# Hybrid decoder block: the state-space scan with channels on the partitions, and its norm applied after the output product

## The chip, the cores and the metric

One NeuronCore of a Trainium2 chip runs the whole program. Its engines are TensorE (PE in the rows), VectorE (DVE), ScalarE (ACT), GpSimd (POOL) and SyncE (SP, which issues most DMAs). The metric is the time on the device in microseconds (us) for one execution, the median of several runs.

## The reference

One decoder layer over 512 positions with a width of 1024: a norm, one projection `w_in` to the columns of three mixers (a convolution, a sparse attention, a state-space scan), their outputs side by side through `w_out`, a residual add, a second norm and a feed-forward part. Only the scan is touched. Its reference, cut to what matters:

```python
CHUNK = 128   # 4 chunks; 8 heads of 64 channels; 2 groups of B and C; state 128
xd  = xh * dt[..., None]
cs  = cumsum(dt * a) within the chunk
scores = (C[l] . B[s]) * exp(cs[l] - cs[s])          # l >= s, per head
y_diag = einsum("bclsh,bcshp->bclhp", scores, xd)
y_off  = einsum("bclhn,bchpn,bclh->bclhp", C, state_before_chunk, exp(cs))
y = y_diag + y_off + d_skip[:, None] * xh
y = rms_norm(y.reshape(S, 512) * silu(z), ssm_norm_g)   # mean over the 512 channels
x = x + concat([conv, att, y], -1) @ w_out
```

## The kernel before, in words

Everything is float32. The large products are done in three passes of a rounded part (`_hi`) and its rest (`_lo`): weight high by input high, weight high by input low, weight low by input high (`product`, L1767). A weight of 128 by 2048 numbers is a "chunk"; ScalarE makes `w_hi` of it (L934) and VectorE `w_lo` (L640), in two slots that alternate.

The order of work is one list, `PLAN`, made by `make_plan`. It has four "slots" for each of the 23 chunks before the feed-forward part. A slot begins with TensorE's 12 matmuls of a quarter of a chunk (`mg`), and the plan puts small steps at fixed slots. Every engine walks the same list and does its part of each step, so that its instructions stay in that order; semaphores join the engines. In a slot, the steps of `front` stand first, then those of `put`, then those of `fill`.

The scan takes one chunk of 128 positions (t = 0 to 3) each four slots, from n = 68, 72, 76 and 80 (`SSD_SLOTS`). The steps of one chunk are:
- `csr` (n): TensorE spreads the running sum `cs` over the partitions, four heads in a bank (bfloat16, L2000 and L2005).
- `seg` (n+1): ScalarE takes `dec` = exp of it, eight instructions of 128x128 (L1099). GpSimd makes `xd`, `xskip` (the D skip term) and `xdd` (L887 to L892).
- `ssd` (n+1): TensorE makes the product of B and C (`gt2`, L2014) and turns B round (`bt`, L1773).
- `sct` (n+2): VectorE makes the scores, `gt2` by `dec` (L1463).
- `yd` (n+2): TensorE multiplies scores and `xd` (L2031): for each head the 128x128 scores are the stationary operand and 64 columns of `xd` move, so that positions come out on the partitions. From t = 1 on it multiplies C and `state` (`yo`, L2039), and up to t = 2 it makes the next state (`st`, L2047).
- `ssdout` (n+3): VectorE scales `yo` by exp(cs), adds `yd` and `xskip`, multiplies by silu(z) (L1490) into `yb`, and updates `state`.
- `ysq`, `yms` (n+3, n+4), `yn`: ScalarE sums the squares along each row with an accumulator (L1114), VectorE and GpSimd make the inverse root, and VectorE scales `yb` by it and by the norm's gain `gssm` (L1512).
- `yT`, `ssdT` (n+5, n+6): TensorE turns `yb` so that channels are on the partitions (L1773), ScalarE takes `ssm_hi` (L922) and VectorE `ssm_lo` (L1519).

From slot 68 to 91 the large products are those with `w_out`: att in two halves, conv in two halves, ssm in two halves, four `mg` each. VectorE adds each to the residual `x2` (step `wo`, L1575), and the second norm follows. `z`, the gate of the scan, is projected in slots 60 to 67 with `h` stationary, two chunks of four k tiles each, positions on the partitions.

Results pass through eight PSUM banks. Four (`acc`) serve the large products, three (`aux`) the small steps in rotation, one (`out`) `pv` and `yd`. A step claims its bank, and waits until the group that had it before has been drained:

```python
        def claim(eng, *key):
            if RING[key][3]:
                eng.wait_ge(drained[RING[key][2]], RING[key][3])
```

## Time and profile before

| | us |
|---|---|
| median of 3 runs | 717.45 (717.26 to 717.74) |
| the profiled execution | 717.7 |
| its span in the profile | 716.0 |
| TensorE busy | 697.0 (97%) |
| VectorE busy | 545.4 (76%) |
| ScalarE busy | 380.6 (53%) |
| GpSimd busy | 141.8 (20%) |

The span is the time from the first to the last instruction of the profile; 1.7 us of the execution lie around it. The granted TensorE clock is full in all 40 slices of the page. The scan lies between about 275 and 352 us of the span, the feed-forward part begins at about 371 us.

A matmul of float32 operands stands in the trace as two records, so that eight of them are "x16". Matmuls are pipelined: the duration of one is longer than the distance to the next, and what a group of them takes is read from one start to the next.

### The profile page before, as it was taken

The page shows a single profiled execution, that of the slowest core. Times are in us where ns is not written, and L with a number is a line of the kernel's source. Part 1 is how long each engine was busy: PE and PEld are TensorE (multiplying, and loading weights), DVE is VectorE, ACT ScalarE, POOL GpSimd, SP SyncE. Part 2 cuts the span into 40 slices and gives each one's busy share as a digit, 9 for nine tenths or more (in the row PEclk, how much of TensorE's full clock was granted, in tenths as well). Part 3 has the DMA queues.
Part 4 walks back from the last instruction along what each step waited for, and adds up shares of the span by engine and source line. Part 5 has one row for each costly group of instructions (what it writes and reads, how often), then busy time and mean ns, then how long its engine had stood idle before and what let it go on. Part 6 is the DMA issues. An engine that isn't in the chain of part 4 may idle for free.

```text
span 716.0 us, 9787 instructions
## 1 busy us (share of the span) xinstructions
PE 697.0 (97%) x3402; PEld 560.4 (78%) x3402; DVE 545.4 (76%) x852; ACT 380.6 (53%) x570; POOL 141.8 (20%) x114
## 2 busy tenths in 40 slices
PE   4999999999999999999999999999999999999998
PEld 4776888667666788788888888888888888888886
DVE  4368989988898947667667777876766866997895
ACT  6254655988878765633464343343343343654660
POOL 2000477944564402233410000000000000000000
PEclk9999999999999999999999999999999999999999
DMA  8731314211111141312234588656687547864552
GB/s 245 235 127 60 118 59 117 62 60 59 59 60 60 59 177 61 135 70 60 59 118 140 173 246 249 190 170 200 186 249 237 179 160 298 297 221 140 169 162 88
DMA packets 87554, 104.09 MB, mean 145 GB/s; under 512 B 6871, under 2 KB 65591, under 8 KB 87519
## 3 DMA queue, kind: packets, MB, share of 16 engines
q1 hardware_dynamic: 87375, 103.12, 45.9%
q10 hardware_dynamic: 144, 0.52, 0.2%
q8 instruction: 20, 0.33, 0.2%
q14 instruction: 15, 0.12, 0.1%
HBM read 87.10 MB, written 16.54 MB: 145 GB/s over the span
## 4 chain that ended last, share of the span: by engine, by line
PE 87%; ACT 7%; DVE 4%; issue 2%; DMA 1%; POOL 0%; DVEq 0%; ACTq 0%
PE bank L1767 75%; PE bank L1773 4%; PE bank L1787 2%; ACT tapped L1129 1%; ACT w_hi L934 1%; PE bank L1975 1%; DVE u_acc L622 1%; PE bank L2031 1%; PE bank L1951 1%; DVE xbcT L1427 1%; PE bank L1926 1%; DMA x_in<-in_x 1%; ACT prob L1052 1%; ACT dec L1099 0%; DVE prob L1406 0%
## 5 line engine op out<-in xcount | busy, mean ns | idle before, releaser
L1767 PE MATMUL bank<-h_hi,w_hi 128*128 128x512 f32 (+1 forms) x496 | 192.9, 389 | 0.0
L1767 PE MATMUL bank<-h_lo,w_hi 128*128 128x512 f32 (+1 forms) x496 | 189.9, 383 | 0.0
L1767 PE MATMUL bank<-h_hi,w_lo 128*128 128x512 f32 (+1 forms) x496 | 189.8, 383 | 0.0
L1767 PEld LDWEIGHTS bank<-h_hi,w_hi 128*128 128x128 f32 x496 | 93.2, 188 | 25.7 <-issue 7.8
L1621 DVE SCALAR_TENSOR_TENSOR f<-bank,prm,f 128x511 f32<-128x511 f32 x88 | 65.8, 748 | 60.7 <-ACT f L1182 55.2
L1767 PEld LDWEIGHTS bank<-h_hi,w_lo 128*128 128x128 f32 x496 | 93.2, 188 | 18.4
L1767 PEld LDWEIGHTS bank<-h_lo,w_hi 128*128 128x128 f32 x496 | 93.3, 188 | 17.3
L860 POOL TENSOR_TENSOR u_acc<-tapped,u_acc 128x511 f32<-128x511 f32 (+29 forms) x60 | 90.1, 1502 | 46.1 <-ACT tapped L1129 43.0
L1182 ACT ACTIVATE f<-bank,prm 128x512 f32<-128x512 f32 x44 | 34.2, 777 | 70.4 <-PE bank L1767 70.2
L640 DVE TENSOR_TENSOR w_lo<-w_raw,w_hi 128x2048 fp32r<-128x2048 f32 x24 | 55.6, 2316 | 8.9 <-ACT w_hi L934 8.7
L1767 PE MATMUL bank<-w_hi,g_parts 128*128 128x512 f32 x168 | 53.8, 389 | 0.0
L1596 DVE TENSOR_TENSOR w_lo<-w_raw,w_hi 128x2048 fp32r<-128x2048 f32 x22 | 50.3, 2287 | 3.4 <-ACT w_hi L1171 3.4
L622 DVE SCALAR_TENSOR_TENSOR u_acc<-u_in,prm,u_acc 128x511 f32<-128x511 f32 (+29 forms) x60 | 51.9, 877 | 0.8
L1189 ACT ACTIVATE sg<-f 128x512 f32<-128x512 f32 x22 | 13.9, 632 | 72.4 <-DVE f L1621 72.4
L1129 ACT ACTIVATE tapped<-u_in,prm 128x511 f32<-128x511 f32 (+29 forms) x60 | 40.2, 704 | 21.4 <-POOL u_acc L860 15.5
L1767 PE MATMUL bank<-w_hi,h_hi 128*128 128x512 f32 x128 | 51.2, 400 | 0.0
L1767 PE MATMUL bank<-w_hi,h_lo 128*128 128x512 f32 x128 | 50.0, 390 | 0.0
L1767 PE MATMUL bank<-w_lo,h_hi 128*128 128x512 f32 x128 | 49.9, 390 | 0.0
L934 ACT ACTIVATE w_hi<-w_raw 128x2048 fp32r<-128x2048 f32 x24 | 45.8, 1910 | 3.5 <-DMA w_raw<-in_w_in 2.2
L840 POOL TENSOR_TENSOR stats<-stats 128x1 f32<-128x1 f32 (+1 forms) x24 | 23.1, 966 | 103.4 <-DVE stats L1507 35.1
L1171 ACT ACTIVATE w_hi<-w_raw 128x2048 fp32r<-128x2048 f32 x22 | 41.9, 1906 | 0.0
L1767 PEld LDWEIGHTS bank<-w_hi,g_parts 128*128 128x128 f32 x168 | 31.5, 188 | 6.6
(279 smaller groups left out, 1228.2 us busy)
## 6 DMA issues: line engine op xcount, KB each, us to landing
w_raw<-in_w_up SPq DMA_DIRECT2D x44, 512.0 KB, 6.1
w_raw<-in_w_in SPq DMA_DIRECT2D x34, 512.0 KB, 4.6
down_raw<-in_w_down SPq DMA_DIRECT2D x22, 512.0 KB, 5.4
weight_sums<-down_raw SPq DMA_DIRECT2D x11, 768.0 KB, 5.3
w_raw<-in_w_out SPq DMA_DIRECT2D x12, 512.0 KB, 4.5
weight_sums<-w_sum SPq DMA_DIRECT2D x11, 512.0 KB, 2.7
w_raw<-weight_sums SPq DMA_DIRECT2D x6, 768.0 KB, 6.0
down_raw<-weight_sums SPq DMA_DIRECT2D x5, 768.0 KB, 4.4
```

Of the source, the lines that this page charges most:

```text
L622: eng.scalar_tensor_tensor(out=u_acc[:, j, i:], in0=u_in[:, j, 0:SEQ - i], scalar=w, in1=u_acc[:, j, i:], op0=ALU.mult, op1=ALU.add).then_ ...
L640: eng.tensor_tensor(wlo[:, slot, cols], wraw[:, slot, cols], whi[:, slot, cols].bitcast(F32), ALU.subtract).then_inc(ready, 1)
L840: pool.tensor_tensor(out_, in_, half_neg[:, 0:n], ALU.pow).then_inc(ready, 1)
L860: pool.tensor_tensor(u_acc[:, j, i:], tapped[j][:, i % 4, 0:SEQ - i], u_acc[:, j, i:], ALU.add).then_inc(dw_taps[j], 1)
L934: act.activation(whi[:, c % NSLOT, :], wraw[:, c % NSLOT, :], ACT.Copy)\
L1129: act.activation(tapped[j][:, i % 4, 0:SEQ - i], u_in[:, j, 0:SEQ - i], ACT.Copy, scale=prm[:, c:c + 1]).then_inc(dwp_ready, 1)
L1171: act.activation(whi[:, c % NSLOT, :], wraw[:, c % NSLOT, :], ACT.Copy)\
L1182: act.activation(fbuf[:, 2 * s + v, :], bank[FFN_BANK[2 * s + v]][:, :], ACT.Identity, bias=prm[:, bass.ds(tile + R_FB, 1)], scale=prm[:, ...
L1596: dve.tensor_tensor(wlo[:, c % NSLOT, :], wraw[:, c % NSLOT, :], whi[:, c % NSLOT, :].bitcast(F32), ALU.subtract)\
L1621: ins = dve.scalar_tensor_tensor(out=fbuf[:, 2 * s + v, i:], in0=bank[FFN_BANK[2 * s + v]][:, 0:SEQ - i], scalar=prm[:, bass.ds(tile + (R_ ...
L1767: ins = pe.matmul(o, a, b, start=first and i == 0 and q == 0, stop=last and i == n - 1 and q == 2)
L1773: return pe.transpose(o, in_, ident[0:n, 0:n])
```

## The change

The scan is computed with channels on the partitions throughout, and the norm's factor, which belongs to a position, is applied later, where positions are on the partitions again.
- `yd`: `xd` of one head (128x64) is stationary and the scores (128x128) move. The two heads of a pair write the two halves of the bank's partitions. `yo`: `state` is stationary and C moves, four matmuls of 128 columns.
- `eb`, new from t = 1 on: TensorE spreads cs over the partitions of the channels (eight bfloat16 matmuls, 64 partitions by 128 columns), ScalarE takes exp of it into `ecs_rows`. This takes the place of the scaling by a column of `ecs`. Its bank is in the rotation of three.
- `xskip` is made by four GpSimd instructions of 128x128 from `xbcT`, no longer by one of 128x512; `dcol` (two small copies on VectorE) holds the factors.
- `z` is projected as two chunks of all eight k tiles, with `w` stationary, channels on the partitions. Its loads have rows of 256 numbers, not 512.
- `ysq`: ScalarE squares `yb` without an accumulator and takes `ssm_hi` = `yb` by the gain, from SBUF, four instructions (the gain is one number for each partition). `yred` (VectorE) sums the squares of the four channel tiles, `yq` (TensorE, 32 columns) sums over the partitions, `yms` (VectorE, GpSimd) makes the inverse root, one slot later than before. `ssm_lo` takes four instructions from SBUF.
- `yT`, `yn` and the turning are gone. The inverse root scales the ssm product at the residual add (`wo`, ssm), eight instructions.
- The gain arrives as four rows of `prm` instead of a row spread over all partitions.

The core of the diff:

```diff
-        put(n + 4, ("yms", t))
-        front[n + 5].append(("yn", t))
-        put(n + 5, ("yT", t))
-        front[n + 6].append(("ssdT", t))
+        front[n + 4] += [("yred", t), ("ssdT", t)]
+        put(n + 5, ("yq", t))
+        front[n + 6].append(("yms", t))
...
+            if s[1]:
+                aux.append(("eb", s[1]))
...
-            if what in ("iq", "xbc", "conv"):
+            if what in ("iq", "xbc", "z", "conv"):
...
-                    pool.tensor_tensor(sk3, v3, per_head(hbc[:, 2, :]), ALU.mult)\
-                        .then_inc(xd_ready, 1)
-                    pool.wait_ge(xd_ready, 3 * t + 1)
+                    for j in range(4):
+                        pool.tensor_scalar(xskip[:, P * j:P * j + P], xbcT[:, j, P * t:P * t + P],
+                                           dcol[:, j:j + 1], None, ALU.mult).then_inc(xd_ready, 1)
+                    pool.wait_ge(xd_ready, 6 * t + 1)
...
+                    if t:
+
+                        if t > 1:
+                            evacuated(act, "yo", t - 1)
+                        finished(act, "eb", t)
+                        drain(act.activation(ebc[:, :], ps("eb", t)[:, :], ACT.Exp), "eb", t)
...
-                    act.activation(dump[:, :], yb[:, :], ACT.Square,
-                                   accum_out=yss[:, t:t + 1]).then_inc(yss_ready, 1)
-                elif k == "ssdT":
-                    t = s[1]
-                    finished(act, "yT", t)
-                    high(ssm_hi[:, :, P * t:P * t + P],
-                         ps("yT", t)[:, :].rearrange("p (j q) -> p j q", j=4))
+                    act.activation(dump[:, :], yb[:, :], ACT.Square).then_inc(ysq_ready, 1)
+                    for j in range(4):
+                        act.activation(ssm_hi[:, j, P * t:P * t + P], yb[:, P * j:P * j + P], ACT.Copy,
+                                       scale=prm[:, R_SG + j:R_SG + j + 1]).then_inc(shi_ready, 1)
...
-                    dve.wait_ge(yss_ready, t + 1)
-                    dve.tensor_scalar(yss[:, t:t + 1], yss[:, t:t + 1], 1.0 / 512, EPS, ALU.mult,
-                                      ALU.add).then_inc(yms_ready, 1)
-                elif k == "yn":
-                    t = s[1]
-                    dve.wait_ge(yrs_ready, t + 1)
-                    dve.scalar_tensor_tensor(out=yb[:, :], in0=yb[:, :], scalar=yrs[:, t:t + 1],
-                                             in1=gssm[:, :], op0=ALU.mult, op1=ALU.mult)\
-                        .then_inc(yn_ready, 1)
+                    finished(dve, "yq", t)
+                    drain(dve.tensor_scalar(yss[:, t:t + 1], ps("yq", t)[:, 0:1], 1.0 / 512, EPS,
+                                            ALU.mult, ALU.add), "yq", t)
+                    evacuated(dve, "yq", t)
+                    dve.sem_inc(yms_ready, 1)
                 elif k == "ssdT":
                     t = s[1]
-                    wait_high(s)
+                    dve.wait_ge(shi_ready, 4 * t + 4)
                     q = slice(P * t, P * t + P)
-                    drain(dve.tensor_tensor(ssm_lo[:, :, q],
-                                            ps("yT", t)[:, :].rearrange("p (j q) -> p j q", j=4),
-                                            ssm_hi[:, :, q].bitcast(F32), ALU.subtract), "yT", t)
+                    for j in range(4):
+                        dve.scalar_tensor_tensor(
+                            out=ssm_lo[:, j, q], in0=yb[:, P * j:P * j + P],
+                            scalar=prm[:, R_SG + j:R_SG + j + 1], in1=ssm_hi[:, j, q].bitcast(F32),
+                            op0=ALU.mult, op1=ALU.subtract).then_inc(slo_ready, 1)
+                elif k == "yred":
+                    t = s[1]
+                    dve.wait_ge(ysq_ready, t + 1)
+                    dve.tensor_reduce(ysq_sum, dump[:, :].rearrange("p (j q) -> p q j", j=4),
+                                      AX_X, ALU.add).then_inc(yred_ready, 1)
...
-                    drain(dve.tensor_tensor(xx, ps(*s)[:, :], xx, ALU.add), *s)
+                    if g == "ssm":
+
+                        dve.wait_ge(yrs_ready, t + 1)
+                        drain(dve.scalar_tensor_tensor(out=xx, in0=ps(*s)[:, :],
+                                                       scalar=yrs[:, t:t + 1], in1=xx,
+                                                       op0=ALU.mult, op1=ALU.add), *s)
...
+                    if t:
+                        claim(pe, "eb", t)
+                        for j in range(4):
+                            for n in range(2):
+                                c = SH * t + 2 * j + n
+                                ins = pe.matmul(
+                                    ps("eb", t)[SP_ * n:SP_ * n + SP_, P * j:P * j + P],
+                                    sel3[:, c:c + 1].to_broadcast([96, SP_]), cs_rows[:, :],
+                                    start=True, stop=True)
+                        ins.then_inc(aux_done, 1)
...
-                        c = slice(SP_ * h, SP_ * h + SP_)
-                        ins = pe.matmul(ps("yd", t)[:, c], sct[:, h, :], xd[:, c], start=True,
+                        j, n = divmod(h, 2)
+                        ins = pe.matmul(ps("yd", t)[SP_ * n:SP_ * n + SP_, P * j:P * j + P],
+                                        xd[:, SP_ * h:SP_ * h + SP_], sct[:, h, :], start=True,
                                         stop=True)
...
+                elif k == "yq":
+                    t = s[1]
+                    pe.wait_ge(yred_ready, t + 1)
+                    claim(pe, "yq", t)
+                    pe.matmul(ps("yq", t)[:, 0:32], ysq_sum, ones[:, 0:32], start=True, stop=True)\
+                        .then_inc(aux_done, 1)
```

TensorE from `yd` of t = 1 to `yd` of t = 2, in the order before (the 24 matmuls of two slots, `csr`, and 12 and 12 more stand where rows are left out):

```order
L2031 MATMUL bank<-xd,sct 128x64 x8
L2039 MATMUL bank<-state,xbcT 128x256 x2
L2047 MATMUL bank<-xdd,b_tok 128x256 x2
...
L1773 MATMUL bank<-ident,yb 128x128 x4
L2014 MATMUL bank<-xbcT 128x128 x2
L1773 MATMUL bank<-ident,xbcT 128x128 x2
...
L2031 MATMUL bank<-xd,sct 128x64 x8
```

And in the order of the change (`cs_rows,sel_55` after `bt` is `eb`, `ones,stats` is `yq`):

```order
L2069 MATMUL bank<-sct,xd 64x128 x8
L2078 MATMUL bank<-xbcT,state 128x128 x4
L2086 MATMUL bank<-xdd,b_tok 128x256 x2
...
L2093 MATMUL bank<-ones,stats 128x32
L2042 MATMUL bank<-xbcT 128x128 x2
L1799 MATMUL bank<-ident,xbcT 128x128 x2
L2055 MATMUL bank<-cs_rows,sel_55 64x128 x8
...
L2069 MATMUL bank<-sct,xd 64x128 x8
```

The turning of `yb` gives way to one matmul, and the eight of `eb` are put in between `bt` and the next `mg`.

VectorE from the gate of t = 1 to the scores of t = 2, before (`x_115` is `x2`):

```order
L1490 TENSOR_TENSOR yb<-yb,z_tok 128x512
L1496 TENSOR_TENSOR state<-state,stats 128x512
L1500 TENSOR_TENSOR state<-bank,state 128x512
L1575 TENSOR_TENSOR x_115<-bank,x_115 128x512
L1507 TENSOR_SCALAR stats<-stats 128x1
L1575 TENSOR_TENSOR x_115<-bank,x_115 128x512
L1512 SCALAR_TENSOR_TENSOR yb<-yb,stats,gssm 128x512
L1575 TENSOR_TENSOR x_115<-bank,x_115 128x512
L640 TENSOR_TENSOR w_lo<-w_raw,w_hi 128x2048
L1519 TENSOR_TENSOR ssm_lo<-bank,ssm_hi 128x4x128
L1463 TENSOR_TENSOR sct<-bank,dec 128x512 x2
```

And in the change:

```order
L1506 TENSOR_TENSOR yb<-yb,z_tok 128x512
L1512 TENSOR_TENSOR state<-state,stats 128x512
L1516 TENSOR_TENSOR state<-bank,state 128x512
L1601 TENSOR_TENSOR x_115<-bank,x_115 128x512
L1539 TENSOR_REDUCE stats<-square_dump 128x128
L1532 SCALAR_TENSOR_TENSOR ssm_lo<-yb,prm,ssm_hi 128x128 x4
L1601 TENSOR_TENSOR x_115<-bank,x_115 128x512 x2
L645 TENSOR_TENSOR w_lo<-w_raw,w_hi 128x2048
L1523 TENSOR_SCALAR stats<-bank 128x1
L1480 TENSOR_TENSOR sct<-bank,dec 128x512 x2
```

`ssm_lo` has moved from between `w_lo` and `sct` to ahead of `w_lo`; `yms` (the TENSOR_SCALAR that reads a bank) stands behind `w_lo` and drains the bank of `yq`.

ScalarE from the square of t = 0 to `dec` of t = 1, before:

```order
L1114 ACTIVATE square_dump,stats<-yb 128x512
L1150 ACTIVATE u_tok<-bank,prm 128x4x128
L1155 ACTIVATE conv_hi<-u_tok 128x512
L1150 ACTIVATE u_tok<-bank,prm 128x4x128
L1155 ACTIVATE conv_hi<-u_tok 128x512
L934 ACTIVATE w_hi<-w_raw 128x2048
L1099 ACT_TABLE_LOAD
L1099 ACTIVATE dec<-bank,stats 128x128 x8
```

And in the change:

```order
L1129 ACTIVATE square_dump<-yb 128x512
L1131 ACTIVATE ssm_hi<-yb,prm 128x128 x4
L1164 ACTIVATE u_tok<-bank,prm 128x4x128
L1169 ACTIVATE conv_hi<-u_tok 128x512
L1164 ACTIVATE u_tok<-bank,prm 128x4x128
L1169 ACTIVATE conv_hi<-u_tok 128x512
L941 ACTIVATE w_hi<-w_raw 128x2048
L1106 ACT_TABLE_LOAD
L1106 ACTIVATE dec<-bank,stats 128x128 x8
```

The four instructions of `ssm_hi` are new in this stretch; they came after `dec`, as one, before.

## Rows read from the trace of the kernel before

**Rows 1.** The page: span; busy time and share of the engines.

```profile
span 716.0 us, 9787 instructions
PE 697.0 (97%) x3402; PEld 560.4 (78%) x3402; DVE 545.4 (76%) x852; ACT 380.6 (53%) x570; POOL 141.8 (20%) x114
```

**Rows 2.** Windows: stretch, then busy us of each engine, clock, DMA share, GB/s.

```profile
262.00:371.00 109.00, 107.15 (x596) 89.68 (x595) 76.02 (x117) 56.78 (x106) 31.68 (x28) 1.00 0.26 83
371.00:716.00 345.00, 341.76 (x1542) 284.09 (x1540) 260.68 (x324) 148.28 (x162) 0.00 (x0) 1.00 0.62 195
```

**Rows 3.** Timeline of TensorE, t = 0 and 1: start, us, what, [idle before].

```profile
283.56 0.39 PE L1767 MATMUL bank<-w_hi,att_lo 128*128 128x512 f32 x1
283.79 1.89 PE L2031 MATMUL bank<-xd,sct 128*128 128x64 f32 x16
285.52 1.08 PE L2047 MATMUL bank<-xdd,b_tok 128*128 128x256 f32 x4
...
298.83 0.44 PE L1773 MATMUL bank<-ident,xbcT 128*128 128x128 f32 x2 [0.32 <-ACT dec L1099]
...
301.63 0.39 PE L1767 MATMUL bank<-w_hi,att_lo 128*128 128x512 f32 x1
302.15 2.00 PE L2031 MATMUL bank<-xd,sct 128*128 128x64 f32 x16
303.98 1.08 PE L2039 MATMUL bank<-state,xbcT 128*128 128x256 f32 x4
304.90 1.03 PE L2047 MATMUL bank<-xdd,b_tok 128*128 128x256 f32 x4
...
316.00 0.48 PE L1767 MATMUL bank<-w_hi,conv_hi 128*128 128x512 f32 x1
```

**Rows 4.** Chain that ended last: start, us from this to the next, what.

```profile
249.19 1.02 PE bank L1975 x16
...
261.41 0.22 PE bank L1993 x2
...
311.64 0.23 PE bank L2005 x4
...
335.76 1.73 PE bank L2031 x16
...
346.63 0.44 PE bank L1773 x4
```

**Rows 5.** Timeline of ScalarE, from the first turned conv tile to `dec` of t = 1.

```profile
287.08 0.78 ACT L1150 ACTIVATE u_tok<-bank,prm 128x512 f32<-128x512 f32 x1 [2.23 <-PE bank L1773]
...
289.76 0.61 ACT L1114 ACTIVATE square_dump<-yb 128x512 f32<-128x512 f32 x1
...
290.71 0.78 ACT L1150 ACTIVATE u_tok<-bank,prm 128x512 f32<-128x512 f32 x1 [0.24 <-PE bank L1773]
...
295.31 1.28 ACT L1099 ACT_TABLE_LOAD   x1
296.60 2.17 ACT L1099 ACTIVATE dec<-bank,stats 128x128 f32<-128x128 f32 x8
```

**Rows 6.** Timeline of VectorE, t = 1 to 2.

```profile
305.17 0.69 DVE L1476 TENSOR_TENSOR yb<-bank,stats 128x512 f32<-128x512 f32 x1 [2.48 <-PE bank L2039]
...
312.74 2.53 DVE L640 TENSOR_TENSOR w_lo<-w_raw,w_hi 128x2048 fp32r<-128x2048 f32 x1
...
317.79 1.28 DVE L1463 TENSOR_TENSOR sct<-bank,dec 128x512 f32<-128x512 f32 x2
```

**Rows 7.** Groups of VectorE by shape: count, busy us, mean ns, idle before.

```profile
L1374 DVE TENSOR_REDUCE stats<-sq 128x8 f32<-128x512 f32 x8 | 5.4, 678 | 3.4 <-ACT sq L1021 3.4
L1512 DVE SCALAR_TENSOR_TENSOR yb<-yb,stats,gssm 128x512 f32<-128x512 f32 x4 | 5.3, 1332 | 0.2
L1547 DVE SCALAR_TENSOR_TENSOR x2n<-x,stats,gf_row 128x512 f32<-128x512 f32 x4 | 3.0, 749 | 0.8 <-POOL stats L840 0.7
```

**Rows 8.** Timelines of GpSimd (t = 1), VectorE and TensorE (the end of the stage).

```profile
293.74 1.49 POOL L892 TENSOR_TENSOR xdd<-xd,stats 128x512 f32<-128x512 f32 x1
...
356.85 0.68 DVE L1575 TENSOR_TENSOR x<-bank,x 128x512 f32<-128x512 f32 x1
...
362.34 1.09 PE L1773 MATMUL bank<-ident,x2n 128*128 128x128 f32 x8 [0.77 <-ACT x2n L1141]
```

More of the change, by code:

```diff
@@ L38 @@
 R_QG, R_KG = 96, 97
-N_ROW0 = 98
+R_SG = 98
+N_ROW0 = 102
 R_CW = N_ROW0
@@ L466, in build @@
                   2: at("tapped2", [P, 4, 512], F32, r1)}
-        gssm = at("gssm", [P, 512], F32)
+        ebc = at("ecs_rows", [P, 512], F32)
         dec = at("dec", [P, SH, P], F32, rs)
@@ L654, in load @@
                 done = w_landed[c % NSLOT]
-                if what in ("iq", "xbc"):
-                    c0 = C_IQ if what == "iq" else C_XBC + 256 * i
+                if what in ("iq", "xbc", "z"):
+                    c0 = {"iq": C_IQ, "xbc": C_XBC, "z": C_Z}[what] + 256 * i
                     src = w_in[:, c0:c0 + 256].rearrange("(k p) n -> p k n", p=P)
@@ L880, in _ @@
                     v3 = xs_tok[:, t, :].rearrange("p (h c) -> p h c", h=SH)
-                    x3, xx3, sk3 = (b_.rearrange("p (h c) -> p h c", h=SH)
-                                    for b_ in (xd[:, :], xdd[:, :], xskip))
+                    x3, xx3 = (b_.rearrange("p (h c) -> p h c", h=SH)
+                               for b_ in (xd[:, :], xdd[:, :]))
                     def per_head(ap):
@@ L1883, in _ @@
                             pe.wait_ge(pool_lo_ready, POOL_LO.index(c) + 1)
-                    if what in ("iq", "xbc", "conv"):
+                    if what in ("iq", "xbc", "z", "conv"):
                         key = ("cg" if q < 2 else "ca", i) if what == "conv" else \
@@ L1900, in _ @@
                         key, k0 = ("wo", g, half, q), 0
-                        if half == 0 and g != "conv":
-                            evacuated(pe, "pv" if g == "att" else "yT", q)
+                        if half == 0 and g == "att":
+                            evacuated(pe, "pv", q)
+                        elif half == 0 and g == "ssm":
+                            pe.wait_ge(slo_ready, 4 * q + 4)
                         elif (half, q) == (0, 0):
```

66 lines of the change are left out of this document (36 added, 30 removed).

## The prediction

> **What bounds the kernel now.** I read the page first: TensorE is busy for 697.0 of 716.0 us [rows 1], so time is won or lost where TensorE's instructions become fewer or shorter, or where it waits. Next the windows: the feed-forward part from 371 us on has 341.8 busy us in 345 and no step of the change; the stretch 262 to 371, where the scan lies, has 107.15 in 109 [rows 2]. So in this stage too TensorE is the engine that the others follow, and its waits make up under 2 us. Then the timelines of this stage, which show where these waits are. At t = 0 `yd` starts 0.23 us after the last large matmul, which is the usual distance. At t = 1 it starts 0.52 us after it, 0.29 late, and the group then takes 1.83 us to the start of `yo`, not 1.73: a wait costs 0.40 in all [rows 3]. What it waits for is `sct`; at t = 2 that ends at about 319.07, when TensorE starts `yd` at once [rows 6], so the wait is there twice (t = 1 and 2). A third is at 298.83, 0.32 us for `dec` of t = 1 [rows 3]. `dec` is late because ScalarE has worked almost without a break since 287.08: four conv tiles, a square, a `w_hi`, a table load, eight exps [rows 5].
>
> **The change on TensorE, start to start.**
> - `yd`: before, 16 records take 1.73 us [rows 4], 0.108 each although only 64 columns move. After, 64 columns are stationary, 128 move, and the heads alternate between the two halves of the output partitions. This form is in the trace: `pv` of the last block has 64 columns of `v_tok` stationary, 128 moving and alternating halves, and 16 records take 1.02 us [rows 4]. I take 1.02: minus 0.71 each. The bound from above is 1.73 (nothing gained).
> - `yo`: 4 records of 256 columns in 0.92 us (303.98 to 304.90, [rows 3]) become 8 of 128 at 0.11, the price of a turned tile (0.44 for four [rows 4]): 0.88. Minus 0.04.
> - `yT` 0.44 goes, `yq` comes: one matmul of 32 columns on 128 stationary ones, as L1993, 0.22 [rows 4]. Minus 0.22 each.
> - `eb`: eight bfloat16 matmuls of 128 columns, three times. Four of `csr` take 0.23 [rows 4], so at most 0.46; if the halves overlap as in `pv`, 0.27. I take 0.30.
> - `z`: 96 matmuls of 512 columns before and after, and the same bytes; `xbc` is projected in the new form already. Nothing, and its banks are claimed later than before. The load of `gssm` that goes is small and early. Nothing.
>
> **What it does to the waits.** `ssm_lo` no longer stands between `w_lo` and `sct`. Before, `w_lo` of t = 2 ends at 315.27 but `sct` starts only at 317.79 [rows 6], as `ssm_hi`, made from the turned tile, has to come first. After, `sct` needs `gt2` (at about 316) and ends near 317.3, a good microsecond before `yd`. So the 0.40 goes at t = 1 and 2.
>
> The wait for `dec` of t = 1 stays, and here the first chunk's gain is lost. ScalarE starts its stretch when TensorE has turned the first conv tiles (287.08, after `yd` of t = 0), now 0.71 earlier. It waits 0.24 at 290.71 [rows 5], which leaves; the accumulator's read (0.19) goes; four `ssm_hi` come, at the price of `dec`, 2.17 / 8 = 0.27 each [rows 5], 1.09. Sum: -0.71 - 0.24 - 0.19 + 1.09 = -0.05. So `dec` ends 0.05 earlier and TensorE goes on 0.05 earlier, whatever it had gained by `yd` and `yT` of t = 0.
>
> Step by step, TensorE against before:
> - start of `yd`(1): -0.05 + 0.30 (`eb`) - 0.29 (wait) = -0.04
> - to the end of `yo`(1): -0.10 (restart) - 0.71 - 0.04, hence -0.89
> - start of `yd`(2): -0.22 + 0.30 - 0.29, hence -1.10; end of `yo`(2): -1.95
> - t = 3, without a wait: -0.22 + 0.30 - 0.71 - 0.04, hence -2.62; `yq`(3) -0.22: -2.84
>
> **The new wait.** `eb`(t) gets the bank of `yq`(t-1), which is free only when VectorE has done `yms`, and that stands behind `w_lo` in its queue. Behind `eb` on TensorE stand the next 12 large matmuls, so each microsecond of lateness is a microsecond of the kernel. Before, from the start of `yb` (305.17) to the end of `w_lo` (315.27) are 10.1 us [rows 6]. Out go the scaling L1512 with its wait and the small operation, 1.65; in come `yred` (0.60 start to start, 0.68 busy as L1374 [rows 7]) and four `ssm_lo`. A quarter of a clean 512 wide instruction (0.75 [rows 7]) is 0.19, the whole is 0.75; near the lower end, as ScalarE's narrow ones are, I take 0.27 each, 1.1. `w_lo` stays. In all 10.15, with `yms` 10.3. TensorE needs the bank at what was 316.00 before [rows 3], less 0.22: 10.6 us after 305.17, and at t = 3, without `bt`, 10.4. That leaves 0.3 and 0.1 us.
>
> GpSimd eats at this. L1512 has a mean of 1.33 us, L1547, the same form, 0.75 [rows 7]: three of its four ran beside GpSimd's `xdd` (one of them at 293.74 [rows 8]) and took about 0.77 more. Now GpSimd starts its work right after the gate and no longer after `yms`, so `xskip` and `xdd` fall on `ssm_lo`. With all of 0.77 on the path, `eb` is late by 0.5 and 0.7; with half of it, by 0.1 and 0.3. As TENSOR_REDUCE and the adds from PSUM in between have one SBUF input, and L1512's 0.77 came from a whole wide instruction, I take the half and charge 0.3 in all (0.4 less what an earlier GpSimd gives back to `w_lo`).
>
> The Trainium skill, page "SBUF — State Buffer", "Who interferes with whom", says that a VectorE instruction with two SBUF inputs contends with a GpSimd one that reads SBUF, and that the one which comes second is blocked for the whole of the other. The old `ssm_lo` had one input in PSUM, the new one has two in SBUF. By that rule the full 0.77 or more falls on the path, and the gain shrinks; it is the third case below.
>
> **The end of the stage.** TensorE waits 0.77 us at 362.34 for the normed tile [rows 8]; the path to it starts from TensorE itself (`w_hi` of the first feed-forward chunk) and so moves with it. On it lies one residual add, which goes from 0.68 [rows 8] to 0.75 [rows 7]: +0.07. The other seven are covered by TensorE's 2.75 us a slot.
>
> **Sum.** -2.84 + 0.30 + 0.07 = -2.5 us. The profiled execution, 717.7 (span 716.0 and 1.7 around it), would be 715.2 with a span of 713.5. The median stands 0.25 lower, 717.45, hence 715.0.
>
> **The rivals.**
> - Second case: the halves don't overlap for `yd`, it stays at 1.73. For it: `pv` is at 1.02 with different operands, and before the change `yd` already moved half the columns for the same price, so a limit other than columns holds. Against: exactly that shape is measured. Then -0.71 falls away for t = 1 to 3, and ScalarE's stretch starts 0.71 later, of which 0.66 reaches `yd`(1): -2.5 + 2.13 + 0.71 = +0.3, 717.8. No change.
> - Third case: the early work of GpSimd makes VectorE late at all of `eb`(2) and `eb`(3), by all of 0.77, and the narrow instructions take 0.35 each and not 0.27 (0.3 more): `eb` is late by 0.8 and 1.0. -2.84 + 1.8 + 0.07 = -1.0, 716.5. For it: the rule above and L1512's three slow ones. Against: the four narrow instructions need not all meet `xdd`, which took 1.49 to itself when it began at 293.74 [rows 8].
> - Fourth, slower: the same wait, from the other end. If a narrow `ssm_lo` costs as much as a wide one (4 x 0.75 = 3.0) and the strided sum of squares twice its row (1.35), the path from 305.17 is 10.3 + 1.9 + 0.75 + 0.77 = 13.7 us, `eb` is late by 3.1 and 3.3, and the result is -2.84 + 6.4 + 0.07 = +3.6: 721.1. It ends slower than before once the path exceeds about 11.9 us. Against: ScalarE's narrow instructions are far below wide ones [rows 5].
> - Fifth: better than forecast. `eb` at 0.23, no late bank, the restart gone for good: -3.1 to -3.3, 714.2. It belongs to the forecast's own range.
>
> **How the numbers follow.** Forecast with its own range, 714.1 to 715.9: 0.60. Third case 0.17 (it runs from 715.9 to 716.8), second 0.13, slower 0.07, something else (a wait that I haven't found, either way) 0.03. Faster or slower counts from 0.2%, 1.4 us, about what a measurement of this kernel can tell. Faster: 0.60, a quarter of the third case and the half of the second in which the pairing works in part (0.04, 0.06), and 0.02 of the rest: 0.72. Slower: 0.07 and 0.01 of the rest. The same: 0.20. Range 713.9 to 717.3: up to most of the third case and the near side of the second.
>
> **What would show it.** `yd` with 16 records in about 1.0 us, three `eb` at about 0.3; no wait before `yd` at t = 1 and 2; a wait for `dec` before `bt` of t = 1 that has grown from 0.32 to about 1.2 us, as TensorE comes there 0.93 earlier and `dec` does not; `yms` ahead of `eb`, or a wait of a few tenths there that names VectorE. The start of the second norm's turning 2.5 us earlier, the feed-forward part as long as before. I am wrong if `yd` takes 1.7, if `eb` waits over 1 us, or if the distance changes outside 275 to 371 us.

## The result

| | us |
|---|---|
| before, median of 7 runs beside it | 717.43 (717.15 to 717.74) |
| changed, median of 7 runs | 719.93 (717.95 to 720.01) |
| ratio | 1.0026, 95% interval 1.0015 to 1.0037 |
| the profiled execution of the changed kernel | 717.95, span 716.1 |

The change costs 2.5 us where I had forecast a gain of 2.5. The seven runs don't scatter, they stand on three levels: 717.95 once, 718.6 twice, 719.9 to 720.0 four times. Later runs of the same kernel also reached 716.3 to 716.7. So the question is not only what the change costs but what costs it in some executions only. The profiled execution stands on one of the levels, and not on that of the median.

### The profile page after: what moved, and what is told of

Read it like the earlier page. It is cut to its first block, busy times and chain, and to the rows that moved or that the text cites. A ratio compares the mean times of both kernels' runs of the same rounds, so it can differ in the third digit from the quotient of the medians.

```text
span 716.1 us, 9887 instructions
## 1 busy us (share of the span) xinstructions
PE 695.6 (97%) x3426; PEld 557.2 (78%) x3430; DVE 547.8 (76%) x866; ACT 384.4 (54%) x581; POOL 141.6 (20%) x126
## 4 chain that ended last, share of the span: by engine, by line
PE 86%; ACT 7%; DVE 4%; issue 2%; DMA 1%; POOL 0%; DVEq 0%; ACTq 0%
PE bank L1793 76%; PE bank L1799 3%; PE bank L1813 2%; ACT w_hi L941 1%; PE bank L2003 1%; DVE u_acc L627 1%; PE bank L1979 1%; ACT tapped L1141 1%; DVE xbcT L1441 1%; PE bank L1954 1%; DMA x_in<-in_x 1%; ACT prob L1059 1%; DVE w_lo L645 1%; PE bank L2069 1%; ACT dec L1106 0%
## 5 line engine op out<-in xcount | busy, mean ns | idle before, releaser
L1793 PE MATMUL bank<-h_hi,w_hi 128*128 128x512 f32 (+1 forms) x528 | 206.1, 390 | 0.0
L1793 PE MATMUL bank<-h_hi,w_lo 128*128 128x512 f32 (+1 forms) x528 | 202.4, 383 | 0.0
L1793 PE MATMUL bank<-h_lo,w_hi 128*128 128x512 f32 (+1 forms) x528 | 202.4, 383 | 0.0
L1793 PEld LDWEIGHTS bank<-h_hi,w_hi 128*128 128x128 f32 x528 | 99.2, 188 | 27.4 <-issue 8.7
L1793 PEld LDWEIGHTS bank<-h_hi,w_lo 128*128 128x128 f32 x528 | 99.2, 188 | 20.0
L1793 PEld LDWEIGHTS bank<-h_lo,w_hi 128*128 128x128 f32 x528 | 99.3, 188 | 18.2
L1793 PE MATMUL bank<-w_hi,h_hi 128*128 128x512 f32 x96 | 38.0, 395 | 0.0
L1793 PE MATMUL bank<-w_hi,h_lo 128*128 128x512 f32 x96 | 37.4, 390 | 0.0
L1793 PE MATMUL bank<-w_lo,h_hi 128*128 128x512 f32 x96 | 37.4, 389 | 0.0
```

The lines of the kernel that those rows point to most:

```text
L1793: ins = pe.matmul(o, a, b, start=first and i == 0 and q == 0, stop=last and i == n - 1 and q == 2)
```

## The profile after

The page. TensorE is busy for 1.4 us less than in [rows 1], though it has more instructions, and though this execution has a stretch at half clock (without that it is 694.7, 2.3 less, in the first run below):

```profile
span 716.1 us, 9887 instructions
PE 695.6 (97%) x3426; PEld 557.2 (78%) x3430; DVE 547.8 (76%) x866; ACT 384.4 (54%) x581; POOL 141.6 (20%) x126
```

The windows of [rows 2]. The feed-forward part is as long as before. The clock of the first stretch is new: 0.98, where it was 1.00.

```profile
262.00:371.00 109.00, 106.46 (x622) 87.17 (x621) 77.93 (x130) 59.92 (x117) 31.40 (x40) 0.98 0.26 83
371.00:716.00 345.00, 341.88 (x1543) 284.21 (x1541) 260.89 (x324) 148.44 (x162) 0.00 (x0) 1.00 0.62 195
```

TensorE's timeline at t = 1, against the middle of [rows 3]. `yd` takes 1.02 to the start of `yo`, the profile names no wait before it, and `gt2` and `bt` wait for `dec`, 0.81 and 0.32:

```profile
297.66 0.71 PE L2042 MATMUL bank<-xbcT 128*128 128x128 f32 x4 [0.81 <-ACT dec L1106]
298.70 0.44 PE L1799 MATMUL bank<-ident,xbcT 128*128 128x128 f32 x2 [0.32 <-ACT dec L1106]
299.06 0.41 PE L2055 MATMUL bank<-cs_rows,sel 96*64 96x128 bf16 x8
299.41 0.50 PE L1793 MATMUL bank<-w_hi,att_hi 128*128 128x512 f32 x1
...
301.31 0.63 PE L1793 MATMUL bank<-w_hi,att_lo 128*128 128x512 f32 x1
301.73 0.63 PE L1793 MATMUL bank<-w_hi,att_hi 128*128 128x512 f32 x1
...
303.96 1.10 PE L2069 MATMUL bank<-sct,xd 128*64 128x128 f32 x16
304.98 1.16 PE L2078 MATMUL bank<-xbcT,state 128*128 128x128 f32 x8
```

The large matmuls behind `eb` start 0.42 apart and not 0.23. The windows say why (the last three numbers: granted clock, DMA share, GB/s):

```profile
299.00:300.00 1.00, 1.00 (x12) 0.74 (x11) 1.00 (x3) 0.83 (x2) 0.00 (x0) 0.96 0.98 293
300.00:301.00 1.00, 1.00 (x4) 0.78 (x3) 0.35 (x1) 0.12 (x1) 0.00 (x0) 0.50 1.02 393
301.00:302.00 1.00, 1.00 (x4) 0.81 (x3) 0.00 (x0) 0.00 (x0) 0.00 (x0) 0.50 1.07 422
...
303.00:304.00 1.00, 1.00 (x6) 0.56 (x4) 0.00 (x0) 0.00 (x0) 0.00 (x0) 0.83 0.07 29
```

For 3.4 us TensorE is granted half the clock (1.2 GHz). The stretch begins at 299.9, 1.2 us after the second part of the wait for `dec` ended. The chain of this execution (its pieces run from end to end, not from start to start) has 4.55 us for the twelve large matmuls there:

```profile
299.13 0.34 PE bank L2055 x8
299.48 4.55 PE bank L1793 x12
304.03 1.02 PE bank L2069 x16
```

## The experiments

Twelve runs, in four parts. "Level" is a group of executions of one kernel within 0.4 us. A theory named in an expectation is explained where it is tested. Each ratio is to the kernel before, run on the same chip beside it.

**The wait for `dec`, and the clock behind it.** First the changed kernel again, without an edit.

> The changed kernel unchanged, to see its executions again. Its profile showed TensorE waiting 0.81 and 0.32 us for dec of t = 1, then a granted clock of half speed from about 299.7 to 303.3 us (12 matmuls in 4.55 us, 2.75 expected). Theory A (the wait lets the clock fall): the profile shows the drop again, right behind that wait, and a run in which the mean clock is 1.0 is about 1.4 to 1.8 us faster than one with 0.998 at otherwise the same speed. Theory B (the drop is chance): it is absent or elsewhere. Neither explains yet why the runs with clock 0.998 stood at 716.1 and at 718.1 us of span and those with 1.0 at 716.7: a second place must differ by about 2 us between executions, and this profile may show it.

Measured: 716.48 (716.27 to 717.93, 11 runs), ratio 0.9989 (0.998 to 0.9998). Ten of eleven executions are at 716.3 to 716.7, and the profiled one is one of these. Its chain has the same waits and the full clock:

```profile
299.20 0.34 PE bank L2055 x8
299.54 2.94 PE bank L1793 x12
```

4.55 against 2.94: the half clock costs 1.6 us at this place, and the time with it is 717.93. This profile, free of both disturbances, serves below to size the terms.

The wait itself, in this undisturbed execution (`yq`, `gt2`, `bt`):

```profile
296.62 0.30 PE L2093 MATMUL bank<-ones,stats 128*128 128x32 f32 x2
297.73 0.71 PE L2042 MATMUL bank<-xbcT 128*128 128x128 f32 x4 [0.81 <-ACT dec L1106]
298.76 0.44 PE L1799 MATMUL bank<-ident,xbcT 128*128 128x128 f32 x2 [0.32 <-ACT dec L1106]
```

Then the wait is taken away: ScalarE makes `w_hi` of the chunk in question one slot later, behind `dec` and not ahead of it, and VectorE its `w_lo` a slot later too (in `make_plan`).

```
-        fill[4 * c - 4].append(("hi", c))
-        fill[4 * c - (2 if c == LATE_LO else 3 if c < UP0 else 4)].append(("lo", c))
+        late = c == CHUNKS.index(("out", ("conv", 0)))
+        fill[4 * c - (3 if late else 4)].append(("hi", c))
+        fill[4 * c - (2 if late or c == LATE_LO else 3 if c < UP0 else 4)].append(("lo", c))
```

> The changed kernel with w_hi of one chunk (the first of conv) moved on ScalarE from ahead of dec(1) to behind it, and its w_lo a slot later. Theory A: ScalarE reaches the exps of t = 1 1.9 us earlier, the wait of 1.1 us in all goes, the clock stays full, and the time is 1.1 + 1.7 = 2.8 us under that of the change: span about 713.3 us, 715.1 in all. Rival B (the drop is not due to the wait): only the 1.1 us go, the clock still falls somewhere: about 716.9. Rival C (the 2 us between executions lie elsewhere): the runs still spread by 2 us.

Measured: 714.85 (714.75 to 715.26, 6 runs), ratio 0.9966 (0.9954 to 0.9978). TensorE has no idle time from 294 to 302, and the clock stays up (0.999 or more in all six). The time is the one that was forecast of the change alone, by coincidence: the forecast had this wait in it. From `yq` to `gt2` TensorE now takes 0.14 and not 1.11, from `gt2` to `bt` 0.53 and not 1.03. So a wait with 1.13 us of idle time cost 1.47 from start to start, which is most of the 1.6 gained.

The reverse: the kernel before, with `dec`(1) made late by two more 128x512 copies on ScalarE ahead of the square at t = 0.

```
+                    if t == 0:
+                        for _ in range(2):
+                            link(act.activation(dump[:, :], yb[:, :], ACT.Copy))
                     act.activation(dump[:, :], yb[:, :], ACT.Square,
```

> The kernel before with two copies of 128x512 more on ScalarE ahead of the square of t = 0 (about 1.1 to 1.3 us), so that dec(1) comes about 0.9 to 1.1 us later and TensorE, which waited 0.32 us at 298.83, waits about 1.3 us. Theory A: the granted clock falls to half behind this wait and the time rises by about 1.0 + 1.7 = 2.7 us, to 720.1. Rival B (the wait alone does not lower the clock, something in the changed order does): plus 1.0 us only, 718.4, clock 1.0.

Measured: 718.40 (718.24 to 718.68, 11 runs), ratio 1.0015 (1.0006 to 1.0024). The waits are nearly those of the changed kernel. The clock was 0.999 or more in all eleven executions; this is what the rival said (718.4), and theory A (720.1) does not hold in this kernel:

```profile
298.38 0.71 PE L2016 MATMUL bank<-xbcT 128*128 128x128 f32 x4 [0.75 <-ACT dec L1099]
...
299.41 0.44 PE L1775 MATMUL bank<-ident,xbcT 128*128 128x128 f32 x2 [0.32 <-ACT dec L1099]
```

So the longer wait alone costs about 1.0 us. A wait of this length was never followed by half clock in this kernel, and in the changed one it was in some executions.

**The changed kernel on other chips, and a cost of 2.1 us.** The next four ran on one chip. The changed kernel again:

> The changed kernel once more. Seen so far: executions at 716.3 to 716.7 (clock 1.0), 717.9 (0.998, a stretch at half clock behind the wait for dec(1)), and in the first series 718.6 (1.0) and 720.0 (0.998), 2.1 us above these two. If the place that costs 2.1 us is a matter of the chip, this series lies wholly in one pair of the levels; if of the execution, both pairs appear. A profile at 718.6 or 720.0 would show the place.

Measured: 719.41 (716.54 to 721.63, 12 runs), ratio 1.0026 (1.0013 to 1.0039). Levels: 716.6 twice, 718.7 four times, 720.2 four times, 721.63 twice. The 718.7 had clocks of 0.999 to 1.0, so half clock can't be its cause. The profiled execution was one at 720.2 and shows the place. TensorE at t = 0, where the changed kernel had been undisturbed so far:

```profile
283.23 0.39 PE L1793 MATMUL bank<-w_hi,att_lo 128*128 128x512 f32 x1
285.79 1.09 PE L2069 MATMUL bank<-sct,xd 128*64 128x128 f32 x16 [2.17 <-issue]
```

In this execution the clock did not fall behind this wait of 2.17 us (1.00 up to 302), but at 302.1, behind the one for `dec`. "issue" says that the profile names no releaser. `yd` waits for `sct`, `xd` and `xdd`, and GpSimd makes the last two. In the same execution:

```profile
280.24 2.36 POOL L896 TENSOR_SCALAR xskip<-xbcT,stats 128x128 f32<-128x128 f32 x4
282.56 3.13 POOL L899 TENSOR_TENSOR xdd<-xd,stats 128x512 f32<-128x512 f32 x1
```

and in the undisturbed one:

```profile
280.20 2.35 POOL L896 TENSOR_SCALAR xskip<-xbcT,stats 128x128 f32<-128x128 f32 x4
282.52 1.04 POOL L899 TENSOR_TENSOR xdd<-xd,stats 128x512 f32<-128x512 f32 x1
```

VectorE's `w_lo` beside it, in the two (disturbed first, then undisturbed):

```profile
282.51 2.28 DVE L645 TENSOR_TENSOR w_lo<-w_raw,w_hi 128x2048 fp32r<-128x2048 f32 x1
```

```profile
282.50 3.21 DVE L645 TENSOR_TENSOR w_lo<-w_raw,w_hi 128x2048 fp32r<-128x2048 f32 x1
```

One of the two instructions stands still for nearly all the time in which the other runs. If `w_lo` comes first, `xdd` ends 0.90 us after `w_lo` and `yd` is 2.1 us late; if `xdd` comes first, `w_lo` takes 0.93 longer and nothing on the path waits for it. Over all profiles in which `xdd` stands behind the narrow `xskip` the starts decide it: where `xdd` starts 0.01 to 0.02 us behind `w_lo` it won (four executions), 0.05 to 0.06 behind it lost (four). This is a race within 0.05 us, and it explains levels 2.1 us apart. It fell out differently from chip to chip: on the chip of the first three experiments all 17 executions of the changed kernel and of the one with the later `w_hi` won it, on this one 10 of 12 lost.

Three more ran beside this one, made before its cause was known. Six bfloat16 matmuls of 384 columns ahead of `yq`(0) fill the wait for `dec`, to hold the clock:

```
+                    if t == 0:
+                        for _ in range(6):
+                            pe.matmul(ps("yq", t)[:, P:4 * P]... , ident_b[:, :], neg_lb[:, :]... )
```

> The changed kernel with six bfloat16 matmuls of 384 columns (about 0.16 us each) on TensorE ahead of yq(0), in columns of its bank that nobody reads. They fill 1.0 of the 1.1 us that TensorE waits for dec(1). Theory A' (the clock falls because TensorE has little to do from 296.6 to 299.4: a wait in two parts with only small matmuls between): no execution has the half clock, all are at the level of the clock 1.0, 716.4 (or 718.6 where the chip adds 2.1), plus 0 to 0.1. Rival (chance, or something other than the wait): it falls in as many executions as in the unchanged one.

Measured: 718.62 (718.49 to 720.00, 8 runs), ratio 1.0023 (1.0013 to 1.0033). The wait ahead of `gt2` is filled; the clock fell in 2 of 8 executions, against 6 of the 10 in the run beside it that had lost the race. That is too few executions to show that the fill helps, and it leaves the other wait open: all eight lost the race, and the last run of this part shows that the clock can fall behind the wait of the race as well.

`eb` as four matmuls with 128 stationary columns, from a table that GpSimd spreads once, not eight with 64:

```
-                        for j in range(4):
-                            for n in range(2):
-                                c = SH * t + 2 * j + n
-                                ... sel3[:, c:c + 1].to_broadcast([96, SP_]), cs_rows[:, :] ...
+                        for j in range(4):
+                            c = SP_ * (SH * (t - 1) + 2 * j)
+                            ... sel_w[:, c:c + P], cs_rows[:, :] ...
```

> The changed kernel with eb as four matmuls on 128 stationary columns instead of eight on 64 (a wider selection matrix, made by GpSimd in idle time). Theory S (going back from matmuls on 64 stationary columns to full ones costs TensorE 0.15 to 0.2 us each time: the 12 large ones behind eb took 2.94, not 2.77 to 2.83): eb goes from 0.34 to 0.23, the 12 behind it from 2.94 to 2.83, together 0.22 three times, 0.7 us off the unchanged one of the same level: 715.7. Rival (the 2.94 come from the new operands or from bfloat16): 2.94 stays and only 0.3 us go, 716.1.

Measured: 717.82 (715.59 to 719.35, 12 runs), ratio 1.0011 (1.0002 to 1.0019). The median is that of a mixture; read by levels it is 715.6, 717.7, 719.2, each some 0.9 below the changed kernel's, where 0.7 was expected and 0.3 by the rival. Its chain, where the changed kernel has 0.34 and 2.94:

```profile
299.12 0.23 PE bank L2063 x4
299.34 2.80 PE bank L1801 x12
```

And with the later `w_hi` too:

> The two mends together: w_hi of that chunk behind dec(1), and eb in full width. Theories A and S: no wait for dec(1), no half clock, 0.7 us less than the first mend alone (714.85): 714.15, 3.2 under the kernel before. Rival: once the wait is gone GpSimd's added copy or VectorE holds eb, and it stays at 714.8.

Measured: 716.22 (716.01 to 717.82, 11 runs), ratio 0.9992 (0.9983 to 1.0001), so 2 us above what was expected: six executions at 716.0 to 716.2, five at 717.6 to 717.8. The race is why; by these times all eleven lost it. The profiled one (717.61) waited 2.17 us for `yd`(0) and nowhere for `dec`(1), and here the clock fell right behind that first wait, for 3.4 us:

```profile
285.00:286.00 1.00, 0.52 (x7) 0.55 (x9) 0.00 (x0) 0.00 (x0) 1.00 (x2) 0.82 0.42 31
286.00:287.00 1.00, 1.00 (x13) 0.94 (x10) 0.00 (x0) 0.00 (x0) 0.78 (x1) 0.50 0.80 266
```

**The race, tested.** Four runs on a third chip. The base:

> The changed kernel again, as the base of this call. Theory (a race for a shared path): in its profiles so far GpSimd's xdd(0) and VectorE's w_lo start within 0.06 us of each other (282.4 to 282.6). Where xdd(0) starts at most 0.02 us behind, it takes 1.04 us and w_lo 3.21; where it starts 0.05 us or more behind, w_lo takes 2.28 and xdd(0) 3.13, and yd(0) starts 2.17 us later. So the times should fall on levels 2.1 us apart (716.5 and 718.6), each again with 1.4 more where the granted clock halves behind the wait for dec(1): 717.9 and 720.0. Rival (the 2.1 us has another cause, such as instruction fetch, and the long xdd is only its shadow): the levels appear just the same, and the next three runs tell.

Measured: 719.25 (718.55 to 720.10, 6 runs), ratio 1.0030 (1.0018 to 1.0043): three at 718.6, three at 720. Every execution lost the race.

GpSimd's order is turned, so that `xdd` no longer stands behind the four narrow `xskip`:

```
+                    pool.wait_ge(xd_ready, 6 * t + 1)
+                    pool.tensor_tensor(xx3, x3, ...)                    # xdd
                     for j in range(4):
                         pool.tensor_scalar(xskip[:, P * j:P * j + P], ...)
-                    pool.wait_ge(xd_ready, 6 * t + 1)
-                    pool.tensor_tensor(xx3, x3, ...)
...
-                    pe.wait_ge(xd_ready, 6 * t + 6)                     # yd
+                    pe.wait_ge(xd_ready, 6 * t + 2)
```

> The changed kernel with xdd issued ahead of the four narrow xskip instructions on GpSimd, and yd waiting for xdd alone. Race theory: xdd(0) runs at 280.2 to 281.2, ahead of w_lo at 282.5, so yd(0) is never late: every time is 716.5 or, with the half clock behind the wait for dec(1), 717.9; none at 718.6 or 720.0; the median falls from e7's by 0 to 3.4 us. The collision moves to xskip(0), which then ends at about 285.3 to 285.7, in time for yb(0). Rival (another cause): levels at 718.6 and 720.0 stay, with yd(0) 2.17 us behind the last large matmul though xdd(0) took 1.04.

Measured: 716.28 (716.13 to 717.66, 11 runs), ratio 0.9987 (0.9978 to 0.9996). None at 718.6 or 720, beside a base with nothing else; the rival (another cause) is refuted. Two of the eleven are at 717.6 with half clock, which this edit does not touch. The collision has moved to `xskip`, as expected. VectorE waits for it, but starts `yb`(0) when the undisturbed execution does (285.63, there behind the longer `w_lo`), so it costs nothing:

```profile
280.07 1.05 POOL L896 TENSOR_TENSOR xdd<-xd,stats 128x512 f32<-128x512 f32 x1
281.10 4.48 POOL L899 TENSOR_SCALAR xskip<-xbcT,stats 128x128 f32<-128x128 f32 x4
```

```profile
285.68 0.69 DVE L1499 TENSOR_TENSOR yb<-bank,xskip 128x512 f32<-128x512 f32 x1 [1.16 <-POOL xskip L899]
```

Both repairs (this one and the later `w_hi`):

> Both repairs: xdd ahead of xskip on GpSimd, and w_hi of the chunk behind t=0 one slot later, so that neither yd(0) nor dec(1) is waited for. Race theory together with the one that the clock falls only behind a wait: one level, 714.9 (what the later w_hi alone gave on a chip where the race was never lost), clock 0.999 to 1.0 in every execution. Rival: 716.9 in some executions (the 2.1 us has another cause), or 716.3 (the clock falls without the wait).

Measured: 714.60 (714.49 to 714.87, 5 runs), ratio 0.9963 (0.9949 to 0.9976). One level, the clock at 0.999 or more in every execution.

And the race brought about in the kernel before, by two more wide `xskip` on GpSimd at t = 0 (they write the same values again):

```
+                    if t == 0:
+                        for _ in range(2):
+                            link(pool.tensor_tensor(sk3, v3, per_head(hbc[:, 2, :]), ALU.mult))
```

> The kernel before, with two more copies of its wide xskip instruction (128x512, 1.04 us each) ahead of xdd(0) on GpSimd, t=0 only; the output is the same. It makes xdd(0) late by 2.1 us (from 281.5 to 283.6), behind the start of w_lo at 282.8. Race theory: one of the two runs while the other stands still, so that xdd(0) ends at 286.0 to 286.9, yd(0) starts 2.2 to 3.1 us later than 283.79, and the time is 719.6 to 720.5 (with 1.5 more where the clock falls behind that wait). Rival (no shared path, each has its own duration): xdd(0) ends at 284.65, yd(0) is 0.9 us late, 718.3.

Measured: 723.85 (723.56 to 724.05, 4 runs), ratio 1.0091 (1.0076 to 1.0106). The wait is the one expected of the race theory, and the rest is the clock:

```profile
286.53 3.65 PE L2034 MATMUL bank<-xd,sct 128*128 128x64 f32 x16 [3.03 <-issue]
289.97 2.02 PE L2050 MATMUL bank<-xdd,b_tok 128*128 128x256 f32 x4
```

```profile
283.34 3.09 POOL L895 TENSOR_TENSOR xdd<-xd,stats 128x512 f32<-128x512 f32 x1
```

```profile
287.00:290.00 3.00, 3.00 (x16) 3.00 (x16) 0.00 (x0) 0.00 (x0) 0.00 (x0) 0.50 0.96 337
290.00:292.00 2.00, 2.00 (x7) 1.53 (x6) 1.39 (x2) 0.00 (x0) 0.00 (x0) 0.50 0.02 6
```

`xdd` starts at 283.34 and ends at 286.43, and `yd` starts at 286.53: 3.1 us later than the 283.40 of the other edited kernel before. The two instructions met twice: `w_lo` started at 282.39, 0.05 behind the last `xskip`, and took 3.14 for it, and `xdd` ended 0.90 after `w_lo`. Behind the wait TensorE stays at half clock for 6.8 us, to past 293. The time was outside what I expected (719.6 to 722.0) by two more microseconds: the half clock lasted twice as long as in the changed kernel. Its length was in neither theory. All four executions have the same mean clock, 0.995.

**The best version.** The two repairs and the full-width `eb`:

> xdd ahead of xskip, w_hi of the chunk behind t=0 one slot later, and eb as four matmuls on full 128-column weights from a table that GpSimd spreads once in t=0. e4 and e5 tried the third edit with the race for xdd(0) still open, and their medians can't be read for it; their levels can: e4's lowest is 715.6 where the changed kernel's is 716.3 to 716.5. Theory (a return from 64 to 128 stationary columns costs TensorE 0.14 to 0.2 us each): eb goes 0.34 to 0.22 and the twelve large matmuls behind it 2.94 to 2.80, three times, 0.25 each, so 714.6 - 0.75 = 713.85, on one level. Rival (the return costs nothing, and only the eight short matmuls became four): 0.12 three times, 714.25. Rival (the third copy on GpSimd runs into w_lo or makes xd(1) late): 714.6 or above.

Measured: 713.84 (713.72 to 713.87, 5 runs), ratio 0.9950 (0.9937 to 0.9964). It is 6.1 us faster than the changed kernel's first median and 3.5 faster than before. The chain at t = 1 (`eb`, twelve large ones, `yd`, `yo`):

```profile
297.43 0.23 PE bank L2064 x4
297.65 2.80 PE bank L1802 x12
300.45 1.02 PE bank L2076 x16
301.47 1.09 PE bank L2085 x8
```

## Why the prediction was wrong, point by point

Of the expected gains about half came. Two costs that stand nowhere in the sum are larger than they: `xdd`(0) late on GpSimd, and the half clock behind a wait.

| what | forecast | measured |
|---|---|---|
| the steps on TensorE, `yd`(0) to the end of the second norm's last turned tile | -2.5 | -1.3 |
| `yd`(0) late for `xdd`(0), race lost | 0 | +2.1 |
| half clock behind a wait | 0 | +1.4 to 1.6 |

The first row is (369.48 - 283.66) - (370.91 - 283.79), the undisturbed execution against before. The runs agree: undisturbed executions are at 716.4, 1.0 below before (`yd`(0) itself is 0.2 late in them). Read by their times and clocks, 14 of all 36 executions of the changed kernel won the race, two of them with half clock; 22 lost it, 13 with half clock. 716.4 + 2.1 + 1.4 is 719.9, the median of the first seven.

The undisturbed 716.4 is 1.4 above the forecast and close to the third case's 716.5. That is luck: the cost of that case did not come. Of the 1.2 us by which the first row falls short, 0.6 is `yd` and `yo` (three times 0.21) and 0.5 is `eb` with what stands around it (three times 0.18); 0.1 more at each end of the stage and 0.3 less for the wait that did not come nearly cancel.

- **`yd`** 1.73 to 1.02: right, to 0.01. The second rival (no overlap) is refuted.
- **`yo`, forecast -0.04, became +0.17** by the chain, from end to end: 1.09, where before it took 0.92. Its four matmuls (eight records) have 128 stationary columns and follow `yd`, which has 64. Read from start to start the same loss stands in two places: `yo` takes 1.00, and `yd` starts 0.32 behind the last large matmul, not 0.23. By both readings `yd` and `yo` together gained 0.54, not 0.75.
- **`eb`, forecast 0.30**, took 0.34 and cost 0.14 more in the group behind it by the chain (2.94 against 2.80 in the best version). From `bt`(1) to `yd`(1), start to start, the kernel with both repairs takes 3.60 and the best version 3.34: 0.26 less for each `eb`, and three times that is the 0.76 between 714.60 and 713.84 (on two chips). I had summed durations and left out what a change of width between two groups costs. How much of the 0.26 is the width and how much the eight matmuls in place of four no run separates; the 0.09 by which the group's start is late, here and at `yd`, is paid before its own first matmul.
- **`yq`**: 0.14, forecast 0.22, but `gt2` behind it took 0.53, before 0.45. Right in sum.
- **The wait for `sct` at t = 1 and 2**: gone, right. Of the 0.40 only the 0.09 above is left.
- **The wait for `dec`(1)**: its size was right (0.81 + 0.32 = 1.13, forecast "about 1.2"), and so was the sentence that the first chunk's gain is lost in it. The step that failed is the one that stops there: I priced a wait of 1.1 us at its own length, and it can bring half a clock with it (+1.4 to 1.6). The edit that removed it gave 1.6 us (716.48 to 714.85, one chip), at full clock on both sides: 0.5 more than the idle time, 0.34 of it because TensorE starts more slowly behind each part of the wait.
- **ScalarE's stretch**: four `ssm_hi` 1.17, forecast 1.09, and from the start of `yd`(0) to the turned conv tiles TensorE takes 1.99 where before it took 2.65, 0.66 less and not 0.71. `dec` of the undisturbed execution ends 0.07 later against `yd`(0), forecast 0.05 earlier.
- **The new wait of `eb` for `yms`**: forecast up to 0.3 in all; there is none. The four `ssm_lo` took 1.17 (forecast 1.1), `yred` 1.12 (forecast 0.68; the strided sum took more than the row it was priced by). From the start of `yb`(1) to the end of `yms` are 10.36 us, where the sum without GpSimd had 10.3, and the bank was free 0.39 us ahead of `eb`(2) (315.49) and 0.17 ahead of `eb`(3):

```profile
309.44 1.12 DVE L1539 TENSOR_REDUCE stats<-square_dump 128x128 f32<-128x512 f32 x1
310.47 1.17 DVE L1532 SCALAR_TENSOR_TENSOR ssm_lo<-yb,prm,ssm_hi 128x128 fp32r<-128x128 f32 x4
...
312.76 2.28 DVE L645 TENSOR_TENSOR w_lo<-w_raw,w_hi 128x2048 fp32r<-128x2048 f32 x1
314.96 0.14 DVE L1523 TENSOR_SCALAR stats<-bank 128x1 f32<-128x1 f32 x1
```

  What failed is GpSimd's part of this term: `xdd` started only when `ssm_lo` of t = 1 and 2 had ended (311.70 after 311.64, 328.07 after 328.01). At t = 0 they met, and `ssm_lo` took 1.96 us, 0.79 more, as the third case priced it, but nothing on the path waited there. The fourth rival, the slower one, put its cost in this wait. It had the right sign for the wrong reason.
- **The end of the stage**: +0.19 to the last turned tile, forecast +0.07; the wait for the normed tile grew from 0.77 to 0.88.
- **GpSimd**: the step that failed most. I asked what its earlier work does to VectorE at t = 1 to 3, and never priced the change of `xskip` from one wide instruction to four narrow ones on GpSimd itself, nor looked at t = 0. The trace of before had both halves of it. At t = 0 `xdd` ended before `w_lo` (282.82) began, with 0.3 us between them:

```profile
280.50 1.04 POOL L889 TENSOR_TENSOR xskip<-xs_tok,stats 128x512 f32<-128x512 f32 x1
281.51 1.05 POOL L892 TENSOR_TENSOR xdd<-xd,stats 128x512 f32<-128x512 f32 x1
...
311.63 1.49 POOL L889 TENSOR_TENSOR xskip<-xs_tok,stats 128x512 f32<-128x512 f32 x1
313.08 3.09 POOL L892 TENSOR_TENSOR xdd<-xd,stats 128x512 f32<-128x512 f32 x1
```

  At t = 2 `xdd` met `w_lo` (312.74, 2.53 in [rows 6]) and took 3.09, ending 0.90 after it. That cost nothing there, as it ended at 316.17 and `yd`(2) began at 319.13. Four `xskip` take 2.35 where one took 1.04, so `xdd` at t = 0 had to start 1.3 later against `w_lo`, beside its start, with `yd` 0.1 us behind its end. Even where it wins, `yd`(0) starts 0.42 behind the last large matmul and not 0.23, 0.10 of it for `xdd`.

I had quoted the Trainium skill, page "SBUF — State Buffer", "Who interferes with whom", for the third rival: the instruction that comes second is blocked for the whole of the other. The trace agrees but for a tenth of a microsecond (`xdd`, 1.04 by itself, took 3.13 and ended 0.90 after `w_lo`), but I had applied it in one direction only, to VectorE blocked by GpSimd. The rule is symmetric, and the long one of the two was VectorE's.

What stays open is the clock. Half clock came in 2 of the 14 executions that won the race and in 13 of the 22 that lost it, so it came more often with the race lost, and it need not all belong to the wait for `dec`. In the one profile of a lost execution with half clock it fell behind `dec`; the kernel without that wait shows that it can fall behind the race's wait too (5 of 11). For the others it isn't known. The two executions at 721.63 (clock 0.995), which no profile caught, have the time and the clock of both waits halving it once each (718.65 + 2 x 1.5); that is an estimate, not shown.

Why the same wait is followed by half clock in one execution and not in the next is open too, and why the 1.07 us of the edited kernel before never was. One difference is that the next weights are loaded later there (DMA share 0.08 in 300 to 301, where the changed kernel has 1.02); no run tests it. The loads alone don't do it: the undisturbed execution has the same share at full clock, and in the last experiment on the kernel before the clock fell between 286.4 and 286.6 at a share of 0.06. With neither wait (the later `w_hi` where the race was won, both repairs, and the best version, 16 executions) the clock did not fall. Whether filler matmuls hold it is not shown.

## What to carry to other kernels

For an instruction that becomes several narrow ones, price it on its own engine and ask what stands behind it there, at the first pass of the loop too, where the neighbours are other ones. Before pricing an engine's move at nothing, lay the long instructions of VectorE and GpSimd side by side in time: two such as `w_lo` and `xdd`, which take all their inputs from SBUF, hold each other up for nearly their whole length, and an order by 0.05 us decides which. When executions of one kernel fall on levels, look for a race and for the granted clock, and profile more than one of them; and make a wait of TensorE go away altogether, since it can cost more than its length.

## What the runs showed of the hardware

- A wait of TensorE of 1.13 us in two parts was followed by 3.4 us at half clock in some executions only (4 of the 25 in which no other wait stood before it). A wait of 2.17 us was followed by 3.4 us of it in one of four profiles, one of 3.03 us by 6.8 us. In none of the 14 profiles did the clock fall without a wait just before.
- A VectorE instruction of 128x2048 with two inputs in SBUF and a GpSimd one of 128x512 that start within 0.06 us of each other run one after the other: 2.28 and 3.13 us, or 3.21 and 1.04.
- Eight bfloat16 matmuls on 64 stationary columns between groups of 128 cost TensorE 0.26 us more than four on 128. A group on 64 columns starts 0.32 us behind a large matmul where one on 128 starts 0.23 behind it.
- The scan's product with 64 columns stationary and 128 moving, in alternating halves, took 1.02 us, with 128 stationary and 64 moving 1.73.
- Four GpSimd instructions of 128x128 took 2.35 us at the least, one of 128x512 1.04; four on VectorE took 1.17 (one wide 0.75), four on ScalarE 1.17.
